# A modulation in part ahead of the first norm and in part between the projections

## The chip, the cores and the metric

The kernel runs on one core of a Trainium2 chip. The metric is the time of one execution on the device in microseconds (us).
## What is computed

Two layers of a backbone over 512 latent tokens and 256 context tokens of 1024 channels, in fp32. Each layer norms its tokens, scales and shifts them by a modulation (six vectors of 1024 for each of two layers, from the condition c for the latent and from c_ctx for the context tokens), mixes them, and adds the result; then the same with a feed-forward part. Layer 0 mixes by a two-directional recurrence over time (RWKV-7), layer 1 by attention. Cut to what matters here:

```python
mod_lat = einsum('bd,lde->lbe', silu(c), mod_w) + mod_b      # mod_w: (2 layers, 1024, 6144)
mod_ctx = einsum('d,lde->le', silu(c_ctx), mod_w) + mod_b
sh_m, sc_m, gt_m, sh_f, sc_f, gt_f = split(mod_lat[i], 6)    # and the same of mod_ctx
a = rms_norm(h, norm_mix[i]) * (1 + sc_m) + sh_m
xx = 0.5 * (previous token + next token of a) - a            # latent and context apart
xr, xw, xk, xv, xa, xg = (a + xx * mu[j] for j in range(6))
r, k, v = xr @ wr, xk @ wk, xv @ wv                          # and three small products of xw, xa, xg
```

## The kernel before

The program is a row of functions, each with its own block of instructions for every engine; at a block's end all engines meet at a barrier. Tokens are kept by channel: 8 channel tiles of 128 partitions, with 768 tokens (256 context, 512 latent) along the row.

`setup` (L113) issues 21 small loads on SP (the identity, the masks of the recurrence, the rows of parameters), and TensorE turns the parameter rows when all are there.

`modulation` (L178) goes over all of `mod_w` in 24 blocks of 512 columns (2 MB each, three buffers). Every block is split in two fp32r parts: ScalarE rounds it (`modw_hi`, L265), VectorE subtracts (`modw_lo`, L285). TensorE multiplies both parts, 16 matmuls of 512 columns, with the conditions as a stationary operand of four columns (L243, L244), ScalarE copies the result's rows, TensorE folds and turns them by channel (`fold`, L234), and VectorE adds the bias (L279). At the end VectorE makes all eight gains.

`load_tokens` (L309) loads the tokens by row (3 MB), turns them on TensorE with two pairs of banks in turn, copies them by channel, and spills them to DRAM. `norm_whole` (L354) takes the squares on ScalarE, sums them over the channels by matmuls with ones (L377), takes root and reciprocal, scales on VectorE and writes the normed tiles on ScalarE.

`rwkv_inputs` (L526) first makes the shifted difference `xx` of all tiles on VectorE (L675 to L681). Then three rounds follow: eight 128-column tiles of one large product and one small product each, 27 units. The order of the work is written out in `schedule` (L565), which every engine runs through with its own methods: `load` (SP, the weights two units ahead), `split` (ScalarE rounds, VectorE subtracts the weights of the next unit), `mix` (VectorE mixes a tile, L696, ScalarE rounds it, L719, GpSimd subtracts, L743), `product` (TensorE, 48 matmuls in three fp32r passes, L521 to L523) and `finish` (VectorE and ScalarE copy the result out of the banks, L702 and L724; SP waits for both copies, L634 and L635, and writes the tile to DRAM, L636). The mixes of an operand's first use stand ahead of its product; those of the next small product go along with the large one.

`recurrence` (L784) runs over head pairs; SP's `load(0)` at L1030, the load of `gate_w` behind it. After it come the output product, the feed-forward part, the attention, and another feed-forward part, whose weights pass through `SplitWeights` (L490) too.

Of the kernel before, what the change touches and what calls it, by code (L numbers as in the profile page):

```python
# [112 lines left out]
def setup(c, d):  # L113

    nc = c.nc
    with ExitStack() as ctx:
        rows = [ctx.enter_context(nc.sbuf_tensor(f"par_rows{n}", [P, P], F32)) for n in range(3)]
        loaded = ctx.enter_context(nc.semaphore("setup_loaded"))
        turned = ctx.enter_context(nc.semaphore("par_turned"))
        copied = ctx.enter_context(nc.semaphore("par_copied"))  # L120
        gated = ctx.enter_context(nc.semaphore("cond_silu"))
        row_of = lambda a: a.rearrange("(m p) -> m p", p=P)
# [11 lines left out]
        n_loads = 6 + sum(len(x) for x in lists)  # L134
        with nc.Block() as block:
            @block.sync
            def _(sp):
                for t, s in ((c.ident, "k_ident"), (c.ones_head, "k_ones_head"),
                             (c.score_mask, "k_score_mask"), (c.keep, "k_keep")):
                    sp.dma_start(t[:], d[s]).then_inc(loaded, 16)  # L140
                for h in range(2):
                    sp.dma_start(c.level_mask[half(h)], d["k_level_mask"][half(h)][:, :, :, half(h)]).then_inc(loaded, 16)
                for tile, parts in zip(rows, lists):
                    at = 0
                    for part in parts:
                        n = part.shape[0]
                        sp.dma_start(tile[at:at + n, :], part).then_inc(loaded, 16)
                        at += n

            @block.tensor  # L150
            def _(pe):
                pe.wait_ge(loaded, 16 * n_loads)
                for n, m in enumerate(sizes):
                    pe.transpose(c.bank[n][:, 0:m], rows[n][0:m, :], c.ident[0:m, 0:m]).then_inc(turned, 1)

            @block.vector
            def _(dve):
                at = 0
                nc.vector.memset(c.ones[:], 1.0).then_inc(copied, 1)
                nc.vector.memset(c.eps[:, 0:1], 1e-6).then_inc(copied, 1)  # L160
                nc.vector.memset(c.eps[:, 1:2], 64e-5).then_inc(copied, 1)
                dve.wait_ge(turned, 3)
                for n, m in enumerate(sizes):
                    at += CT if n == 2 else 0
                    nc.vector.tensor_copy(c.par[:, at:at + m], c.bank[n][:, 0:m]).then_inc(copied, 1)
                    at += m
                dve.wait_ge(copied, 6)

                nc.vector.tensor_scalar(c.par[:, PLESS:PLESS + CT], c.par[:, PKA:PKA + CT], -1.0, 1.0, ALU.mult, ALU.add)\
                    .then_inc(copied, 1)  # L170

            @block.scalar
            def _(act):
                act.wait_ge(copied, 6)
                nc.scalar.activation(c.cond[:], c.par[:, PC:PC + 16], ACT.Silu).then_inc(gated, 1)

def modulation(c, d):  # L178

    nc = c.nc
    W = 512
    BLOCKS = 2 * 6 * D // W
    BODY = 6
    with ExitStack() as ctx:
        sb = lambda n, s, dt=F32: ctx.enter_context(nc.sbuf_tensor(n, s, dt))  # L190
        sem = lambda n: ctx.enter_context(nc.semaphore(n))
        raw = [sb(f"modw{s}", [P, CT, W]) for s in range(3)]
        hi, lo = ([sb(f"modw_{n}{s}", [P, CT, W], F32R) for s in range(2)] for n in ("hi", "lo"))
        cond, cond_hi = sb("cond_parts", [P, CT, 4], F32R), sb("cond_hi", [P, CT, 4], F32R)
        fold, zeros = sb("fold", [4, 2]), sb("zeros", [P, CT, 4])
        row = [sb(f"modrow{s}", [4, W]) for s in range(2)]
        loaded = [sem(f"modw_loaded{s}") for s in range(3)]
        rounded, rest, product, copied, turned, stored = (sem(f"mod_{n}") for n in (
            "rounded", "rest", "product", "row_copied", "turned", "stored"))
        gains, fold_loaded, parts = sem("norm_gains"), sem("fold_loaded"), sem("cond_parts")  # L200
        src = d["mod_w"].rearrange("l (k p) e -> l p k e", p=P)

        def blocks(eng, step):

            for j in range(BODY):
                step(j, 0, j)
            with eng.Fori(1, BLOCKS // BODY) as i:
                for j in range(BODY):
                    step(BODY * i + j, i, j)

        with nc.Block() as block:
            @block.sync
            def _(sp):
                sp.dma_start(fold[:], d["k_fold"]).then_inc(fold_loaded, 16)
                per = BLOCKS // 2
                for l in range(2):
                    def step(n, cols, j):
                        need(sp, rest, n - 2)
                        sp.dma_start(raw[j % 3][:], src[l][:, :, cols]).then_inc(loaded[j % 3], 16)

                    if l == 0:
                        for j in range(BODY):
                            step(j, slice(j * W, j * W + W), j)
                    with sp.Fori(1 - l, per // BODY) as i:
                        for j in range(BODY):
                            step(per * l + BODY * i + j, bass.ds((BODY * i + j) * W, W), j)

            @block.tensor
            def _(pe):
                def turn(n, s):  # L230
                    pe.wait_ge(copied, n + 1)
                    need(pe, stored, n - 1)
                    for q in range(4):
                        mm = pe.matmul(c.bank[2 + s][:, 2 * q:2 * q + 2], row[s][:, q * P:(q + 1) * P], fold[:],  # L234
                                       start=True, stop=True)
                    mm.then_inc(turned, 1)

                def step(n, i, j):
                    s = j % 2
                    pe.wait_ge(rest, n + 1)  # L240
                    need(pe, copied, n - 1)
                    for k in range(CT):
                        pe.matmul(c.bank[s][0:4, :], cond[:, k, :], hi[s][:, k, :], start=(k == 0), stop=False)  # L243
                        mm = pe.matmul(c.bank[s][0:4, :], cond_hi[:, k, :], lo[s][:, k, :], start=False, stop=(k == CT - 1))  # L244
                    mm.then_inc(product, 1)
                    if not isinstance(n, int) or n:
                        turn(n - 1, 1 - s)

                pe.wait_ge(fold_loaded, 16)
                pe.wait_ge(parts, 4)  # L250
                blocks(pe, step)
                turn(BLOCKS - 1, 1)

            @block.scalar
            def _(act):
                def copy(n, s):
                    act.wait_ge(product, n + 1)
                    need(act, turned, n - 1)
                    signal(act, nc.scalar.copy(row[s][:], c.bank[s][0:4, :]), copied, n + 1)

                def step(n, i, j):
                    s = j % 2
                    act.wait_ge(loaded[j % 3], 16 * (BODY // 3 * i + j // 3 + 1))
                    need(act, product, n - 1)
                    nc.scalar.copy(hi[s][:], raw[j % 3][:]).then_inc(rounded, 1)  # L265
                    if not isinstance(n, int) or n:
                        copy(n - 1, 1 - s)

                blocks(act, step)
                copy(BLOCKS - 1, 1)  # L270

            @block.vector
            def _(dve):
                v = nc.vector

                def finish(n, s):
                    dve.wait_ge(turned, n + 1)
# [1977 lines left out]
```

## Time and profile before

| | us |
|---|---|
| median of 3 runs | 2885.71 (2883.48 to 2888.0) |
| the profiled execution | 2886.92 |
| its span, first to last instruction | 2885.1 |
| TensorE busy in the span | 2454.2 (85%) |
| VectorE busy | 1245.5 (43%) |
| ScalarE busy | 898.8 (31%) |
| GpSimd busy | 457.6 (16%) |
| granted TensorE clock, mean | 0.927 |

The page's first part gives these busy times, its second part the span in 40 slices. The busy share of an engine is a mean over stages that are limited by different things; which engine or transfer a stage waits for is read from that stage's own stretch. A line in a grouped view names the source line, the engine, the operation, output and inputs, shapes and count, then busy time and mean duration, then the idle time before it and what ended it. Matmuls are pipelined: the records of neighbours overlap, and an fp32 matmul that isn't fp32r leaves two records.

### The profile page before, as it was taken

The numbers are of one execution on the slowest core, as the hardware profiler recorded it, in microseconds if no ns is written. First come the engines' busy times: TensorE is split into PE (matmuls) and PEld (weight loads), VectorE is DVE, ScalarE is ACT, GpSimd is POOL, SyncE is SP. The second block draws the span as 40 slices with busy tenths as digits, with TensorE's granted clock in tenths as the row PEclk, the third lists the DMA queues.
The fourth block names the chain that finished last, engine by engine and source line by source line (L and its number), as shares of the span: only waits on it lengthen the run. The fifth ranks groups of instructions, "written<-read, shape, count | busy, mean of one in ns | idle before, by whom it ended". The sixth has DMA issues, their size and how long they took to land. (4 is left out here: it accounts for less than half of the span.)

```text
span 2885.1 us, 60344 instructions
## 1 busy us (share of the span) xinstructions
PE 2454.2 (85%) x26259; PEld 1985.4 (69%) x26259; DVE 1245.5 (43%) x1589; ACT 898.8 (31%) x1342; POOL 457.6 (16%) x335
## 2 busy tenths in 40 slices
PE   4863999759889888988697999999969676899999
PEld 1332877548887777878586888888856343588887
DVE  4656444245555555554234222222227654433333
ACT  4543233233233233332115321122143332443231
POOL 0001233053443444343000000000012000000000
PEclk9886999779999999999898999999989898999999
DMA  7751322200000000000122121222111001233332
GB/s 280 286 195 66 104 83 84 80 20 3 27 21 8 26 21 8 27 8 3 63 96 59 58 74 58 59 65 70 40 45 51 0 0 29 58 98 103 90 100 89
DMA packets 235966, 191.73 MB, mean 66 GB/s; under 512 B 10466, under 2 KB 201580, under 8 KB 235244
## 3 DMA queue, kind: packets, MB, share of 16 engines
q1 hardware_dynamic: 235756, 188.57, 20.6%
q8 instruction: 175, 2.87, 0.4%
q14 instruction: 35, 0.29, 0.0%
HBM read 170.73 MB, written 17.83 MB: 65 GB/s over the span
## 5 line engine op out<-in xcount | busy, mean ns | idle before, releaser
L515 DVE TENSOR_TENSOR ffn_lo<-ffn_raw,ffn_hi 128x1024 fp32r<-128x1024 f32 (+1 forms) x120 | 159.8, 1332 | 575.4 <-ACT ffn_hi L511 575.3
L521 PE MATMUL bank<-operand_hi,ffn_hi 128*128 128x512 f32 (+1 forms) x1056 | 379.3, 359 | 25.4 <-DVE operand_lo L486 25.4
L522 PE MATMUL bank<-operand_lo,ffn_hi 128*128 128x512 f32 (+1 forms) x1056 | 378.5, 358 | 0.0
L523 PE MATMUL bank<-operand_hi,ffn_lo 128*128 128x512 f32 (+1 forms) x1056 | 375.7, 356 | 0.0
L511 ACT CAST ffn_hi<-ffn_raw 128x1024 fp32r<-128x1024 f32 (+1 forms) x120 | 136.5, 1137 | 532.9 <-PE bank L523 532.7
L1472 POOL TENSOR_TENSOR lvl<-sc,level_mask 128x512 f32<-128x512 f32 x144 | 198.2, 1383 | 468.8 <-PE bank L1098 439.1
L521 PEld LDWEIGHTS bank<-operand_hi,ffn_hi 128*128 128x128 f32 x1056 | 200.7, 190 | 62.7 <-issue 22.2
L523 PEld LDWEIGHTS bank<-operand_hi,ffn_lo 128*128 128x128 f32 x1056 | 200.2, 190 | 29.9
L522 PEld LDWEIGHTS bank<-operand_lo,ffn_hi 128*128 128x128 f32 x1056 | 200.9, 190 | 27.3
L521 PE MATMUL bank<-mix_hi,proj_hi 128*128 128x256 f32 (+1 forms) x432 | 153.5, 355 | 56.4 <-POOL mix_lo L743 56.4
L522 PE MATMUL bank<-ffn_g_lo,ffn_hi 128*128 128x512 f32 (+1 forms) x528 | 188.0, 356 | 0.0
L521 PE MATMUL bank<-ffn_g_hi,ffn_hi 128*128 128x512 f32 (+1 forms) x528 | 187.5, 355 | 0.0
L523 PE MATMUL bank<-ffn_g_hi,ffn_lo 128*128 128x512 f32 (+1 forms) x528 | 186.7, 354 | 0.0
L1263 DVE TENSOR_TENSOR inverse<-bank,inverse 128x512 f32<-128x512 f32 x120 | 82.6, 688 | 178.4 <-PE bank L1107 178.1
L743 POOL TENSOR_TENSOR mix_lo<-mix_full,mix_hi 128x768 fp32r<-128x768 f32 (+1 forms) x48 | 87.9, 1832 | 439.4 <-ACT mix_hi L719 438.5
L522 PE MATMUL bank<-mix_lo,proj_hi 128*128 128x256 f32 (+1 forms) x432 | 151.8, 351 | 0.0
L523 PE MATMUL bank<-mix_hi,proj_lo 128*128 128x256 f32 (+1 forms) x432 | 150.2, 348 | 0.0
L1107 PE MATMUL bank<-inverse,t_sb 64*64 64x64 f32 x3840 | 135.3, 220 | 10.5 <-DVE inverse L1263 5.7
L1098 PE MATMUL bank<-inverse_t,lvl 64*64 64x64 f32 x3840 | 142.8, 228 | 0.8 <-DVE inverse_t L1257 0.7
L521 PEld LDWEIGHTS bank<-mix_hi,proj_hi 128*128 128x128 f32 x432 | 85.3, 197 | 76.2 <-issue 38.9
L243 PE MATMUL bank<-modw_hi,cond_parts 128*4 128x512 f32 x192 | 88.8, 463 | 53.5 <-DVE modw_lo L285 53.5
L1107 PEld LDWEIGHTS bank<-inverse,t_sb 64*64 64x64 f32 x3840 | 124.8, 137 | 13.4 <-DVE inverse L1263 6.7
(250 smaller groups left out, 4966.3 us busy)
## 6 DMA issues: line engine op xcount, KB each, us to landing
modw<-in_mod_w SPq DMA_DIRECT2D x24, 2048.0 KB, 8.5
ffn_raw<-in_ff_w SPq DMA_DIRECT2D x88, 512.0 KB, 3.8
ffn_raw<-in_ff_w SPq DMA_DIRECT2D x32, 704.0 KB, 4.6
proj_raw<-in_rw_wr SPq DMA_DIRECT2D x8, 512.0 KB, 3.9
proj_raw<-in_rw_wk SPq DMA_DIRECT2D x8, 512.0 KB, 4.1
proj_raw<-in_rw_wv SPq DMA_DIRECT2D x8, 512.0 KB, 4.0
rwkv_out_raw<-in_rw_wo SPq DMA_DIRECT2D x8, 512.0 KB, 3.6
qk_w_raw<-in_at_wq SPq DMA_DIRECT2D x8, 512.0 KB, 3.6
```

Source lines behind the costliest of these rows:

```text
L243: pe.matmul(c.bank[s][0:4, :], cond[:, k, :], hi[s][:, k, :], start=(k == 0), stop=False)
L511: signal(act, self.nc.scalar.copy(self.hi[s][:, 0:k_tiles, :], self.raw[s][:, 0:k_tiles, :]), self.rounded, n + 1)
L515: signal(eng, eng.tensor_tensor(self.lo[s][:, 0:k_tiles, :], self.raw[s][:, 0:k_tiles, :], self.hi[s][:, 0:k_tiles, :].bitcast(F32), ALU.s ...
L521: pe.matmul(out, w[0], x[0], start=first, stop=False)
L522: pe.matmul(out, w[0], x[1], start=False, stop=False)
L523: return pe.matmul(out, w[1], x[0], start=False, stop=last)
L743: signal(pool, nc.gpsimd.tensor_tensor(column(mix_lo[q % 2], k), full[s][:], column(mix_hi[q % 2], k).bitcast(F32), ALU.subtract), mix_res ...
L1098: mm = pe.matmul(T_BANK[half(h), w * CH:w * CH + CH], lvl[G.parity][n % 2][half(h), w, :], inv_t[G.parity][half(h), w, :], start=True, sto ...
L1107: mm = pe.matmul(X_BANK[half(h), w * CH:w * CH + CH], t_sb[G.parity][half(h), w, :], inv[G.third][half(h), w, :], start=True, stop=True)
L1263: v.tensor_tensor(y, X_BANK[:], y, ALU.add).then_inc(x_added, 1)
L1472: g.tensor_tensor(lvl[G.parity][n % 2][:].rearrange("p (q e) t -> p q e t", e=2), sc[G.third][:, :, :, 0, :], c.level_mask[:, n].unsqueeze ...
```

## The change

- `setup`, `modulation`, `load_tokens` and `norm_whole` become one function, `opening`, and a class `Modulation`. Blocks are 256 columns wide (48 of them, 1 MB each in two pieces of 512 KB) and are multiplied in plain fp32, without a split. The conditions are padded to 32 stationary columns, and the four channel tiles of a piece go to four column groups of the array (`tile_position=(0, 32 * j)`), whose parts are summed by the `fold` matmul when the row is turned.
- `opening` computes only blocks 0 to 7 (shift and scale of layer 0's mixer) ahead of the normed tiles, and blocks 8 and 9 among them.
- The first norm works by token: ScalarE sums the squares of the rows, the rows are scaled and then turned, and gain and shift are applied as they leave the banks. The unscaled tokens are turned too, for the spill, through one pair of banks.
- The other 38 blocks stand in `rwkv_inputs`: 10 to 15 among the first mixes (k < 6), 16 to 47 behind the units, one each and two in units 4, 8, 12, 17, 21 and 25. Every engine does its part of a block at that place in its own order: SP the loads, TensorE the turn of the block before and the product, ScalarE the copy, VectorE the store of the block before. Buffers there: three pieces.
- The shift is made tile by tile, ahead of the tile's first mix. The loops over pairs of units are unrolled.
- The masks of the recurrence are loaded in `recurrence`, behind `load(0)` and ahead of `gate_w`; VectorE and GpSimd wait for them at the start.
- `SplitWeights` has one set of semaphores for all stages, counted on from stage to stage.

```diff
+MOD_W = 256
+MOD_BLOCKS = 2 * 6 * D // MOD_W
+MOD_EARLY = 10
+class Modulation:
+    def load(self, sp, n, i):
+        piece = 2 * (n - self.first) + i
+        need(sp, self.product, piece - self.deep + 1)
+        l, at = n // (MOD_BLOCKS // 2), n % (MOD_BLOCKS // 2) * MOD_W
+        sp.dma_start(self.raw[piece % self.deep][:], self.src[l][:, 4 * i:4 * i + 4, at:at + MOD_W])\
+            .then_inc(self.loaded[piece % self.deep], 16)
+    def multiply(self, pe, n):
+        m = n - self.first
+        need(pe, self.copied, m)
+        for i in range(2):
+            piece = 2 * m + i
+            pe.wait_ge(self.loaded[piece % self.deep], 16 * (piece // self.deep + 1))
+            for j in range(4):
+                mm = pe.matmul(self.c.bank[6][32 * j:32 * j + 32, 0:MOD_W], self.c.cond[:, 4 * i + j, :],
+                               self.raw[piece % self.deep][:, j, :], start=(i == 0), stop=(i == 1),
+                               tile_position=(0, 32 * j))
+            mm.then_inc(self.product, 1)
+    def turn(self, pe, n):
+        m = n - self.first
+        pe.wait_ge(self.copied, m + 1)
+        need(pe, self.stored, m)
+        for q in range(2):
+            mm = pe.matmul(self.c.bank[7][:, 2 * q:2 * q + 2], self.row[:, q * P:(q + 1) * P], self.c.fold[:],
+                           start=True, stop=True)
+        mm.then_inc(self.turned, 1)
...
+def opening(c, d, a, spilled):
...
+        mods = Modulation(c, ctx, d, "mod0", 8)
...
+                sp.dma_start(xt[:, 0:2, :], d["ctx"][0].rearrange("(t p) e -> p t e", p=P)).then_inc(x_loaded[0], 16)
+                sp.dma_start(xt[:, 2:T, :], d["x"][0].rearrange("(t p) e -> p t e", p=P)).then_inc(x_loaded[1], 16)
...
+                for k in range(CT):
+                    need(pe, lat_copied, k)
+                    need(pe, ctx_copied, k)
+                    turn_x(xt, k, (c.bank[0], c.bank[1]), turned)
+                pe.wait_ge(gated, 1)
+                mods.multiply(pe, 0)
+                turn_rows(2)
+                mods.turn(pe, 0)
+                for n in range(1, 8):
+                    mods.multiply(pe, n)
+                    mods.turn(pe, n)
+                    if n == 4:
+                        pe.wait_ge(rows_copied, 2)
+                        turn_scaled(0), turn_scaled(1)
+                for k in range(2, CT):
+                    turn_scaled(k)
+                    if k % 3 == 2:
+                        n = 8 + k // 3
+                        if n < MOD_EARLY:
+                            mods.multiply(pe, n)
+                            mods.turn(pe, n)
...
 def rwkv_inputs
+        mods = Modulation(c, ctx, d, "mod1", 3)
+        mods.first = MOD_EARLY
...
+        AHEAD = 6
+        def mods_after(u):
+            rest = MOD_BLOCKS - MOD_EARLY - AHEAD
+            cuts = [MOD_EARLY + AHEAD + rest * i // (UNITS - 1) for i in range(UNITS)]
+            return list(range(cuts[u], cuts[u + 1])) if u + 1 < UNITS else []
...
             for k in range(CT):
                 E.mix(0, k, k % 2)
+                if k < AHEAD:
+                    E.mod(MOD_EARLY + k)
...
                         E.product(u, 2 * m, 2 * i + s)
                         E.finish(u, m, 2 * i + s)
-                pair(0)
-                with E.eng.Fori(1, CT // 2 - 1) as i:
-                    pair(i)
-                pair(CT // 2 - 1)
+                        for n in mods_after(u.n):
+                            E.mod(n)
...
+                        if k in (2, 5):
+                            for n in mods_after(u.n)[k // 3:k // 3 + 1]:
+                                E.mod(n)
...
                 class Sp(Part):
+                    def mod(self, n):
+                        for i in range(2):
+                            mods.load(sp, n, i)
...
                 class Pe(Part):
+                    def mod(self, n):
+                        if n > MOD_EARLY:
+                            mods.turn(pe, n - 1)
+                        mods.multiply(pe, n)
...
                 class Act(Part):
+                    def mod(self, n):
+                        mods.copy(act, n)
...
                 load(0)
+                sp.dma_start(keep[:], d["k_keep"]).then_inc(masks_loaded, 16)
+                sp.dma_start(score_mask[:], d["k_score_mask"]).then_inc(masks_loaded, 16)
+                for h in range(2):
+                    sp.dma_start(level_mask[half(h)], d["k_level_mask"][half(h)][:, :, :, half(h)]).then_inc(masks_loaded, 16)
                 sp.dma_start(gate_w[:], d["rw_g2"][0]).then_inc(slices[0], 16)
```

## Rows read from the trace of the kernel before

**Rows 1.** Stretches: length; PE, PEld, DVE, ACT, POOL busy; clock; DMA share; GB/s.

```profile
13.40:204.20 190.80, 136.98 (x576) 58.21 (x576) 110.59 (x61) 100.37 (x48) 0.00 (x0) 0.87 0.73 264
204.20:224.20 20.00, 8.27 (x48) 7.33 (x48) 5.53 (x8) 3.00 (x9) 0.00 (x0) 0.66 0.40 158
224.20:255.70 31.50, 12.28 (x32) 6.47 (x32) 12.62 (x9) 18.76 (x27) 0.00 (x0) 0.74 0.24 101
255.70:296.30 40.60, 14.52 (x49) 10.08 (x50) 32.22 (x29) 8.84 (x11) 14.52 (x8) 0.63 0.14 39
296.30:540.30 244.00, 229.58 (x1249) 196.31 (x1247) 97.70 (x88) 73.44 (x97) 73.42 (x40) 0.95 0.31 91
```

**Rows 2.** Groups by line and form within the modulation, 13 to 204 us.

```profile
L285 DVE TENSOR_TENSOR modw_lo<-modw,modw_hi 128x4096 fp32r<-128x4096 f32 x24 | 106.2, 4425 | 50.9 <-ACT modw_hi L265 50.5
...
L234 PE MATMUL bank<-fold,modrow 4*128 4x2 f32 x192 | 25.0, 249 | 0.0
```

**Rows 3.** Timeline of the token load: start, duration, engine, line, what.

```profile
204.22 0.38 SPq L322 DMA_DIRECT2D xt<-in_ctx  x1
...
214.32 1.97 PE L338 MATMUL bank<-ident,xt 128*128 128x128 f32 x8 [11.59 <-DMA xt<-in_x]
...
217.18 0.69 DVE L345 COPY tokens_in<-bank 128x512 f32<-128x512 f32 x1 [0.59 <-PE bank L338]
```

**Rows 4.** The same columns as rows 1, while modulation loads are queued up.

```profile
27.00:32.00 5.00, 2.00 (x5) 0.62 (x6) 4.08 (x2) 3.61 (x1) 0.00 (x0) 1.00 1.05 385
```

**Rows 5.** Timeline of ScalarE in the first norm, each square waiting for TensorE's sums.

```profile
231.00 0.84 ACT L386 ACTIVATE norm_sq<-tokens_in 128x768 f32<-128x768 f32 x1 [0.45 <-PE bank L377]
232.29 0.84 ACT L386 ACTIVATE norm_sq<-tokens_in 128x768 f32<-128x768 f32 x1 [0.45 <-PE bank L377]
```

**Rows 6.** Timeline of TensorE in the recurrence, one group of 64x64 matmuls.

```profile
701.94 1.10 PE L1107 MATMUL bank<-inverse,t_sb 64*64 64x64 f32 x32
```

**Rows 7.** Timeline of VectorE and GpSimd from 255 to 296 us.

```profile
255.81 7.02 DVE L675 TENSOR_TENSOR shifted<-normed 128x766 f32<-128x766 f32 x8 [1.65 <-PEq L367]
...
263.17 7.04 DVE L681 SCALAR_TENSOR_TENSOR shifted<-shifted,normed 128x768 f32<-128x768 f32 x8
...
281.01 3.67 DVE L696 SCALAR_TENSOR_TENSOR mix_full<-shifted,par,normed 128x768 f32<-128x768 f32 x2 [1.92 <-POOL mix_lo L743]
...
295.11 1.02 DVE L696 SCALAR_TENSOR_TENSOR mix_full<-shifted,par,normed 128x768 f32<-128x768 f32 x1
...
279.10 3.71 POOL L743 TENSOR_TENSOR mix_lo<-mix_full,mix_hi 128x768 fp32r<-128x768 f32 x2 [1.88 <-ACT mix_hi L719]
```

**Rows 8.** Timeline of a unit's end: evacuation, write and next load.

```profile
347.31 0.37 ACT L724 COPY proj_out<-bank 128x256 f32<-128x256 f32 x1 [3.42 <-PE bank L523]
347.32 0.69 DVE L702 COPY proj_out<-bank 128x512 f32<-128x512 f32 x1 [4.36 <-PE bank L523]
...
348.04 0.36 SPq L636 DMA_DIRECT2D r_all<-proj_out  x1
348.44 0.43 SPq L506 DMA_DIRECT2D proj_raw<-in_rw_wk  x1
```

**Rows 9.** From the view of the tile proj_raw: its 27 loads.

```profile
DMA to landing us min/median/max: 3.3/4.1/5.1
```

**Rows 10.** Timeline of TensorE in the modulation, after a pause.

```profile
44.69 0.59 PE L243 MATMUL bank<-modw_hi,cond_parts 128*4 128x512 f32 x1 [4.11 <-DVE modw_lo L285]
...
48.56 0.39 PE L243 MATMUL bank<-modw_hi,cond_parts 128*4 128x512 f32 x1
```

**Rows 11.** Timeline of VectorE: evacuations of units 7 and 9.

```profile
355.72 0.69 DVE L702 COPY proj_out<-bank 128x512 f32<-128x512 f32 x1 [4.58 <-PE bank L523]
...
383.87 0.69 DVE L702 COPY proj_out<-bank 128x512 f32<-128x512 f32 x1
```

**Rows 12.** Timeline: the setup's level-mask loads, and ScalarE in the recurrence.

```profile
2.61 1.34 SPq L142 DMA_DIRECT2D level_mask<-in_k_level_mask  x2
...
548.34 0.93 ACT L1397 ACTIVATE tmp<-k_pair,par 128x768 f32<-128x768 f32 x1 [8.28 <-DMA gate_w<-in_rw_g]
```

More of the change, by code:

```diff
@@ L133, in setup, with rows_load @@
         sizes = [114, 120, 32]
-        n_loads = 6 + sum(len(x) for x in lists)
+        LAT_SLOT, CTX_SLOT = slice(0, LAT), slice(0, CTX)
+        def rows_load(eng, n):
+            at = 0
+            for part in lists[n]:
+                eng.dma_start(rows[n][at:at + part.shape[0], :], part).then_inc(rows_loaded[n], 16)
+                at += part.shape[0]
         with nc.Block() as block:
@@ L137, in _ @@
             def _(sp):
[L138 to L148, printed above, removed]
+                sp.dma_start(c.ident[:], d["k_ident"]).then_inc(first_loaded, 16)
@@ L150, in _ @@
+                sp.wait_ge(lat_copied, CT)
+                sp.wait_ge(ctx_copied, CT)
+                sp.dma_start(spilled, h[:]).then_inc(c.spilled, 16)
+                sp.wait_ge(c.spilled, 16)
             @block.tensor
             def _(pe):
[L152 to L270, printed above, removed]
@@ new lines, in turn_rows, with turn_x @@
+                def turn_rows(n):
+                    pe.wait_ge(rows_loaded[n], 16 * (len(lists[n]) + (1 if n == 1 else 0)))
+                    pe.transpose(c.bank[n][:, 0:sizes[n]], rows[n][0:sizes[n], :], c.ident[0:sizes[n], 0:sizes[n]])\
+                        .then_inc(rows_turned, 1)
+                def turn_x(src, k, banks, done):
+                    for t in range(T):
+                        out = banks[0][:, t * P:(t + 1) * P] if t < 2 else banks[1][:, (t - 2) * P:(t - 1) * P]
+                        mm = pe.transpose(out, src[:, t, k * P:(k + 1) * P], c.ident[:])
+                    mm.then_inc(done, 1)
@@ new lines, in _ @@
+                for k in range(2, CT):
+                    dve.wait_ge(turned, k + 1)
+                    v.tensor_copy(h[:, k, CTX:TOK], c.bank[1][:, LAT_SLOT]).then_inc(lat_copied, 1)
+                copy_rows(2, PNM)
+                for n in range(8):
+                    mods.store(dve, n)
+                dve.wait_ge(mods.stored, 8)
+                dve.wait_ge(rows_copied, 2)
+                for r in range(2):
+                    mods.gain(v, 0, 0, PNM, r).then_inc(gains, 1)
+                dve.wait_ge(gains, 2)
@@ new lines, in _ @@
+                act.wait_ge(consts, 4)
+                act.wait_ge(rows_copied, 1)
+                nc.scalar.activation(c.cond[:, :, 0:2].rearrange("p k r -> p r k"),
+                                     c.par[:, PC:PC + 16].rearrange("p (r k) -> p r k", k=CT), ACT.Silu).then_inc(gated, 1)
+                for t in range(T):
+                    if t in (0, 2):
+                        act.wait_ge(x_loaded[t // 2], 16)
+                    nc.scalar.activation(xs[:, t, :], xt[:, t, :], ACT.Square, accum_out=squares[:, t:t + 1]).then_inc(squared, 1)
+                    if t < 2:
+                        act.wait_ge(turned, t + 1)
+                        nc.scalar.copy(h[:, t, 0:CTX], c.bank[0][:, CTX_SLOT]).then_inc(ctx_copied, 1)
@@ new lines, in _ @@
+                act.wait_ge(squared, T)
+                nc.scalar.activation(std[:], squares[:], ACT.Sqrt, scale=1.0 / D, bias=c.eps[:, 0:1]).then_inc(rooted, 1)
+                for k in range(2, 5):
+                    act.wait_ge(turned, k + 1)
+                    nc.scalar.copy(h[:, k, 0:CTX], c.bank[0][:, CTX_SLOT]).then_inc(ctx_copied, 1)
+                act.wait_ge(inverted, 1)
+                for t in range(1, T, 2):
+                    nc.scalar.activation(xs[:, t, :], xt[:, t, :], ACT.Copy, scale=std[:, t:t + 1]).then_inc(scaled_act, 1)
@@ new lines, in _ @@
+                for k in range(5, CT):
+                    act.wait_ge(turned, k + 1)
+                    nc.scalar.copy(h[:, k, 0:CTX], c.bank[0][:, CTX_SLOT]).then_inc(ctx_copied, 1)
+                for n in range(8):
+                    mods.copy(act, n)
+                act.wait_ge(gains, 2)
+                for k in range(CT):
+                    act.wait_ge(s_turned, k + 1)
+                    nc.scalar.activation(a[:, k, 0:CTX], c.bank[2 + 2 * (k % 2)][:, CTX_SLOT], ACT.Identity,
+                                         scale=c.gain[:, 0, 0, 1, k:k + 1], bias=c.mod[:, 0, k, 1:2]).then_inc(a_ctx, 1)
+                    if k % 3 == 2 and 8 + k // 3 < MOD_EARLY:
+                        mods.copy(act, 8 + k // 3)
@@ L569, in schedule @@
                 E.mix(0, k, k % 2)
+                if k < AHEAD:
+                    E.mod(MOD_EARLY + k)
             for m in range(3):
                 base = (CT + 1) * m
-                def pair(i):
+                for i in range(CT // 2):
                     for s in range(2):
@@ L597, in nothing @@
                 pass
-            load = split = mix = product = finish = finish_small = nothing
+            load = split = mix = product = finish = finish_small = mod = nothing
         def column(t, k):
@@ L631, in where @@
                         return m, u.n - m * (CT + 1)
+                    def mod(self, n):
+                        for i in range(2):
+                            mods.load(sp, n, i)
                     def finish(self, u, m, tile):
@@ L705, in _ @@
                 schedule(Dve())
+                mods.store(dve, MOD_BLOCKS - 1)
+                dve.wait_ge(mods.stored, MOD_BLOCKS - MOD_EARLY)
+                for l in range(2):
+                    for kind, base in ((0, PNM), (1, PNF)):
+                        for r in range(2):
+                            if l or kind:
+                                mods.gain(v, l, kind, base, r).then_inc(gains, 1)
             @block.scalar
@@ L1566, in add @@
                 def add(m, s):
[L1567 removed]
+                    dve.wait_ge(w.product, w.at + m + 1)
                     for q, (at, width) in enumerate(segs):
```

329 lines of the change are left out of this document (157 added, 172 removed).

## The prediction

> **What bounds the kernel now.** I read the stages first: the page gives shares of the whole span, so I cut the trace into stretches by stage [rows 1]. After some 13 us of tables, 190.8 us go to the modulation, 20.0 to loading and turning the tokens, 31.5 to the first norm, 40.6 to the start of the time-mix inputs (up to the first projection tile's end at 296.3) and 244.0 to the other 26 products. All engines pass a barrier between these functions, so their lengths add up. The modulation is set by splitting: 24 blocks, one VectorE subtraction of 4.425 us each behind a ScalarE cast that it waits for, 106.2 us busy and 50.9 idle [rows 2]; its matmuls have air. The 244.0 us behind 296.3 are TensorE's: 229.6 busy, at 0.95 of full clock. So time taken from the front counts whole, and whatever is put on TensorE's path between two projections counts whole as well, with what TensorE has to wait for there. Behind the projections stands the recurrence, which the change touches only in when its masks are loaded; the later stages get other semaphore numbers and nothing else, which I cost at nothing.
>
> **The front, shortened.** SP now issues the token loads near 3.5 us. Before, TensorE could use them 10.1 us after the issue [rows 3], so they are there at about 14 us. A channel tile is six transposes (1.3 us a tile: the copy of 0.69 and the 0.59 that it waited [rows 3]) and a copy of 0.69 us, and with one pair of banks instead of two they no longer overlap: with the hand-overs 2.2 us, times 8 = 17.6. Between the second and the third tile VectorE waits for ScalarE's six squares and root, then scales three rows; that holds the banks some 7 us longer. Turned: 14 + 17.6 + 7 = 38.5 us. Only then the first block is multiplied; four blocks have landed long since (385 GB/s were reached with loads queued up [rows 4], 1 MB in 2.7 us), and each later one is asked for when a piece is freed, some 10 us ahead of its use, so DMA is not the bound.
>
> A block is 8 plain fp32 matmuls over 256 columns. The old norm's ones-matmuls show the price of plain fp32: 768 columns in 1.29 us at full clock [rows 5], so 0.43 us each and 3.4 us a block one after the other. The four of a piece lie in different column groups of the array. The nearest row is the recurrence's 64x64 pairs in opposite quadrants: 32 records (16 matmuls of 64 columns, 1.7 us in a row at that price) took 1.10 us with their tail [rows 6], so about two at a time. I take two: 1.7 us a block at full clock, 3.4 at half; bounds 0.85 and 3.4 at full clock. The turning adds a copy (0.37 for that shape [rows 8]), three hand-overs (0.3) and four records of 0.13 (192 took 25.0 us [rows 2]): 1.2 us with nothing beside it, because here the turn follows its own product at once. So 2.9 us a block, 4.8 at half clock, and with TensorE half idle I take 3.8: eight blocks 30, two pairs of scaled transposes 2.4, at 71 us. Then eight channel tiles at 1.3 us with two more blocks among them, less the two tiles turned ahead: 16, and the last parameter rows with the barrier 1.5. The time-mix inputs begin at **88 us** (78 to 102, by the bounds of the block) instead of 255.7. The 3 MB that are spilled go out when the last block's load is issued (near 58) and are done by about 76, so the block's end is not theirs.
>
> **The time-mix inputs to their first product.** VectorE now subtracts the first weight tile ahead of the shift (6.3 us, mostly the wait for the load, which the shift used to cover). A column tile then costs the shift 0.95 + 0.9 + small copies and waits, 2.1 us [rows 7], and the mix 1.0, and GpSimd's 1.85 us come on top, since a VectorE mix beside it takes 1.83 instead of 1.02 us [rows 7]: about 5.1 us a tile. Six blocks (10 to 15) lie between; with three buffers of half a block they turn over in some 5 us and keep pace. 6.3 + 8 x 5.1 + 3 = **50 us** (38 if VectorE and GpSimd didn't hinder each other, 55 if the blocks come last) against 40.6. The first product ends at 88 + 50 = 138 instead of 296.3: **158 us gained** (139 to 180).
>
> **The 32 blocks between the projections: the price.** SP works in order. In a unit it waits for both evacuations of that unit's product, writes the tile out, and *only then* issues the loads of the block that TensorE multiplies right behind that same product. Nothing asks for the block earlier, so its load is exposed each time. From a unit of before: evacuation begins at 347.32, the write is issued at 348.04, the next load at 348.44 [rows 8], 1.2 us after the product's end. A 512 KB load behind such a write lands 4.1 us after its issue (3.3 to 5.1) [rows 9]: the first piece at +5.2, the second 1.4 later at +6.6. TensorE, idle for 5 us, is at half clock then: a pause of 4.11 us was followed by matmuls of 0.59 us, and 3.9 us later they took 0.39 [rows 10]. Two pieces at half clock: 1.7 each, +6.9 and +8.6; the next product runs its first part at half clock, 0.4. So **9.0 us a unit**, over 24 units: 216. Bounds: fastest landing and four matmuls at a time 7.3; one at a time 10.8 (3.4 for the first, 2.1 for the second as the clock comes back). The turn of the block before lies in the wait and costs nothing; without that wait 0.5.
>
> Four of these units (4, 12, 21, 25) carry a second block, whose last piece can be asked for only when the first piece is used up: +3.6 each, 14. In the two small units (8, 17) loads run ahead, as nothing is written there; but the casts of the mix now wait on ScalarE behind a copy that waits for TensorE, and VectorE behind the store. From unit 7's end to unit 9's takes 28.2 us now [rows 11], of which 11 are TensorE waiting for the mixes; with all that chained I get 36.9, +8.7, so they take no more than the 9.0 that unit 7 is charged. Behind ScalarE's copy there queues the rounding of the weights two units on, needed 8 us later: covered. VectorE's store is 0.16 us and SP's later weight load has a unit in hand. Stalls: 216 + 14 = **230 us** (183 to 279).
>
> **The recurrence's start.** Four mask loads (1 MB) now stand between the first pair's slices and the gate weights, and ScalarE's first operation waits for those: 8.28 us after the barrier before [rows 12]. Four issues (1.34 us for the two of the level mask [rows 12], so at most 2.7 in all) and 1 MB at 385 GB/s: 2 to 5, I take **3.5** (0 to 8; not below nothing, as nothing there is taken away).
>
> **Sum.** -158 + 230 + 3.5 = +75.5. Profiled execution 2886.9 (span 2885.1 and 1.8 around it) gives 2962.4; the median of the runs is 1.2 below the profiled one: **2961 us**, 2.6% slower.
>
> **The rivals.** *Four at a time.* The column groups may run together, not by twos. Rows: only pairs are shown. Then 8.5 instead of 9.0 us a unit (-12) and 0.85 us less for ten blocks (-8.5): 2940. The Trainium skill ("TensorE: Matmul & The Clock Gate", Part 3) states this: tiles in different column groups run concurrently, with 2.38 times for three; no run here shows it yet. *One at a time.* Then +1.8 x 24, +1.7 to 2.5 for each of ten early blocks: +63, 3024; a front that stays 25 us longer for other reasons lands near 2990. *Faster: the loads are hidden.* If the next block's data were there when a product ends (the mechanism: SP runs ahead of TensorE by a unit), a block costs its matmuls and turn, 1.7 + 0.5 for 32 = 70: 2887 - 158 + 70 + 3.5 - 1 = 2802. It speaks against it that SP's wait for the evacuation stands ahead of the loads. It decides where the stall falls under (158 - 3.5 - 14) / 24 = 5.9 us a unit, which even the fastest landing (+4.5 for the first piece alone, the second at +5.8, then its matmuls) doesn't reach. *The change doesn't do what it says*: a front that still waits for more than eight blocks; nothing in the diff has it wait so.
>
> **How the numbers follow.** The forecast with matmuls by twos 0.52 (its own range 2925 to 2990), four at a time 0.15, one at a time or a longer front 0.17, hidden loads 0.11, landing and front both at their best ends 0.05 (about 2890 to 2905, no change to slightly slower). A run tells about 0.2% (6 us) from no change. Faster 0.12 (hidden loads and a little of the last), same 0.03, slower 0.85. The range runs from the best ends, 2895, to the one-at-a-time case, 3022, and leaves out the hidden loads and both outer tails.
>
> **What would show it.** In the profile after: projections beginning near 88 us and the first product's end near 138; in the stage behind it TensorE idle for 5 to 6 us ahead of each block's matmuls, released by the DMA of the block's weights; granted clock of that stage well under the 0.95 of now, as each pause ends at half clock; a unit of 17 to 18 us instead of 8.4; the stage 475 us long instead of 244. The starts of the four matmuls of a piece tell whether they run by ones, twos or fours. Pauses under 3 us ahead of the blocks, or SP issuing their loads before the evacuation, would prove the central step wrong; a first product's end after 165 the front.

## The result

The changed kernel takes 2967.1 us, median of four runs (2961.3 to 2971.4), against 2884.6 us beside it: 1.0283 times the time before, 95% interval 1.0263 to 1.0303. The profiled execution, with a span of 2959.5 us, is the fastest of the four, 5.8 us under the median.

Cut by the same stages as rows 1: to the barrier ahead of the time-mix inputs, to the first product's end, to the recurrence's barrier, and to ScalarE's first operation in the recurrence (columns as in rows 1):

```profile
0.00:75.80 75.80, 42.54 (x299) 27.73 (x299) 17.11 (x41) 23.46 (x45) 0.20 (x4) 0.89 0.66 225
75.80:125.00 49.20, 28.00 (x166) 16.67 (x167) 40.95 (x56) 11.13 (x17) 14.53 (x8) 0.62 0.54 161
125.00:615.40 490.40, 339.96 (x1891) 253.83 (x1891) 103.84 (x127) 82.64 (x129) 73.84 (x40) 0.78 0.38 114
615.40:627.35 11.95, 0.00 (x0) 0.00 (x0) 0.91 (x6) 0.00 (x0) 0.00 (x0) 0.54 0.96 274
```

The first product ends at 125.0 instead of 296.3, 171.3 us earlier. The stage behind it is 490.4 us long instead of 244.0 [rows 1], so 246.4 us are lost there. TensorE's idle time in it went from 14.4 to 150.4 us, and its granted clock from 0.95 to 0.78. The two groups that the change put into this stage, and what its matmuls wait for (grouped view of TensorE from 125.0 to 615.4 us):

```profile
L148 PE MATMUL bank<-mod_raw,cond 128*32 128x256 f32 x512 | 65.0, 602 | 140.9 <-DMA mod_raw<-in_mod_w 140.9
...
L159 PE MATMUL bank<-fold,mod_row 128*128 128x2 f32 x131 | 19.4, 252 | 3.2 <-ACT mod_row L168 3.2
```

Who waited longest in the same stretch (engine and line, for whom: us in total, times, longest):

```profile
POOL mix_lo L756 <- ACT mix_hi L729: 393.6, 33, 21.2
ACT mod_row L168 <- PE bank L148: 200.9, 30, 8.8
DVE proj_lo L485 <- ACT proj_hi L480: 191.6, 25, 9.6
PE bank L148 <- DMA mod_raw<-in_mod_w: 140.9, 52, 6.9
```

The first three are engines that stand behind TensorE and are not late. ScalarE's wait for the block is new, and VectorE's wait for ScalarE grew from 30.9 us in the same stretch of before; TensorE itself waits only 5.3 us for GpSimd and 3.2 us for ScalarE here. The fourth is the price.

That closes the account of the stage: 136 us more idle (141 of waiting for the blocks' weights, less 7 of waiting for mixes, and small change), 65.0 and about 19 for the blocks' matmuls and turns, and the products, busy 256 us instead of 229.6: 26 us of half clock. 136 + 65 + 19 + 26 = 246.

One unit shows how (timeline from unit 3's evacuation to unit 4's; the place of rows 8):

```profile
179.64 0.69 DVE L705 COPY proj_out<-bank 128x512 f32<-128x512 f32 x1 [6.38 <-PE bank L494]
...
180.48 0.34 SPq L623 DMA_DIRECT2D r_all<-proj_out  x1
180.87 1.12 SPq L137 DMA_DIRECT2D mod_raw<-in_mod_w  x2
...
185.29 1.08 PE L148 MATMUL bank<-mod_raw,cond 128*32 128x256 f32 x8 [5.40 <-DMA mod_raw<-in_mod_w]
...
186.73 1.08 PE L148 MATMUL bank<-mod_raw,cond 128*32 128x256 f32 x8 [0.35 <-DMA mod_raw<-in_mod_w]
...
197.37 0.69 DVE L705 COPY proj_out<-bank 128x512 f32<-128x512 f32 x1 [5.82 <-PE bank L494]
```

Evacuation, write, and only then the loads; TensorE gets the first piece 5.65 us after the evacuation began, the second at 7.1, and the next product begins at 8.1. Unit to unit it is 17.7 us here. Over the 18 such intervals with one block the mean is 18.2 us instead of 8.4.

### The profile page after: what moved, and what is told of

It reads as the page before. It is cut to its first block and busy times, and to the rows that moved or that the text cites. A ratio compares the mean times of both kernels' runs of the same rounds, so it can differ in the third digit from the quotient of the medians.

```text
span 2959.5 us, 60881 instructions
## 1 busy us (share of the span) xinstructions
PE 2455.8 (83%) x26659; PEld 2000.0 (68%) x26659; DVE 1147.6 (39%) x1611; ACT 810.6 (27%) x1340; POOL 457.8 (15%) x335
## 5 line engine op out<-in xcount | busy, mean ns | idle before, releaser
L148 PE MATMUL bank<-mod_raw,cond 128*32 128x256 f32 x768 | 92.5, 587 | 150.8 <-DMA mod_raw<-in_mod_w 150.7
L492 PE MATMUL bank<-mix_hi,proj_hi 128*128 128x256 f32 (+1 forms) x432 | 167.8, 388 | 10.0 <-POOL mix_lo L756 10.0
L756 POOL TENSOR_TENSOR mix_lo<-mix_full,mix_hi 128x768 fp32r<-128x768 f32 x48 | 88.4, 1841 | 501.8 <-ACT mix_hi L729 501.3
L493 PE MATMUL bank<-mix_lo,proj_hi 128*128 128x256 f32 (+1 forms) x432 | 161.4, 374 | 0.0
L494 PE MATMUL bank<-mix_hi,proj_lo 128*128 128x256 f32 (+1 forms) x432 | 158.7, 367 | 0.0
L148 PEld LDWEIGHTS bank<-mod_raw,cond 128*32 128x32 f32 x768 | 21.6, 138 | 187.1 <-issue 131.7
```

Source lines behind the costliest of these rows:

```text
L148: mm = pe.matmul(self.c.bank[6][32 * j:32 * j + 32, 0:MOD_W], self.c.cond[:, 4 * i + j, :], self.raw[piece % self.deep][:, j, :], start=(i ...
L492: pe.matmul(out, w[0], x[0], start=first, stop=False)
L493: pe.matmul(out, w[0], x[1], start=False, stop=False)
L494: return pe.matmul(out, w[1], x[0], start=False, stop=last)
L756: signal(pool, nc.gpsimd.tensor_tensor(column(mix_lo[q % 2], k), full[s][:], column(mix_hi[q % 2], k).bitcast(F32), ALU.subtract), mix_res ...
```

## The experiments

The theory behind the prediction: the loss is the exposed load of each block, set by SP's order, with half clock as an addition. Its rivals: the loads cost by sharing the DMA engines, wherever they stand; other parts of the edit (unrolled loops, the shift by tile, common semaphores) cost as well; the blocks' matmuls are the price.

**The loads ahead of the wait** (e1). This puts them ahead of the unit's write too; a later experiment tries the write alone.

```diff
 (schedule, in each large unit)
+                        for n in mods_after(u.n):
+                            E.early(n)          # SP alone: the two loads of block n
                         E.finish(u, m, 2 * i + s)
                         for n in mods_after(u.n):
                             E.mod(n)            # SP: nothing for a block already asked for
```

> SP issues a unit's block loads ahead of its wait for that unit's evacuation, everything else as in the changed kernel. Theory (the exposed load is the cost): TensorE's 141 us of waiting for the blocks' weights in the 490 us stage go, the clock stays up (26 us less on the products, 30 less on the blocks' matmuls), about 304 us for the stage and 2781 us in all. Rival (the loads cost because they share the DMA engines with weights and writes): under 60 us gained, over 2900.

Measured: 2784.2 us, 0.9646 of the kernel before (0.9630 to 0.9662); 183 us less than the changed kernel. The stage, then SP and TensorE about one product's end at 198.1 us:

```profile
130.40:438.10 307.70, 285.96 (x1891) 231.63 (x1891) 103.17 (x128) 82.70 (x129) 73.43 (x40) 0.94 0.60 178
```

```profile
198.88 0.34 SPq L632 DMA_DIRECT2D r_all<-proj_out  x1
199.27 0.43 SPq L475 DMA_DIRECT2D proj_raw<-in_rw_wk  x1
...
198.34 1.07 PE L148 MATMUL bank<-mod_raw,cond 128*32 128x256 f32 x16
...
207.85 0.50 PE L159 MATMUL bank<-fold,mod_row 128*128 128x2 f32 x4
208.28 1.07 PE L148 MATMUL bank<-mod_raw,cond 128*32 128x256 f32 x16
```

The stage is 307.7 us (304 expected) at a clock of 0.94; behind the product's end SP has only the write and the next weights to issue, a whole block is one row now, 1.07 us with no wait and ahead of SP's write, and the unit 9.93 us. What is left of waiting, 14.5 us instead of 140.9, comes seven times. The same bytes pass at 178 GB/s instead of 114. So sharing the DMA engines isn't the price; the order is. The change's idea is worth 103 us over the kernel before once two loads stand ahead of one wait.

**The 32 blocks left out** (e4).

```diff
         def mods_after(u):
...
-            return list(range(cuts[u], cuts[u + 1])) if u + 1 < UNITS else []
+            return []
```

> Blocks 16 to 47 are left out (their modulation stays zero), all else as in the changed kernel. Theory (the whole loss sits in what stands behind the units): the stage falls back to about 244 us, 2721 us in all. Rival (unrolled loops, the shift tile by tile or the common semaphores cost something too): the stage stays over 260, over 2740.

Measured: 2718.8 us (ratio 0.942, 0.9398 to 0.9441), and the stage is

```profile
126.80:370.70 243.90, 229.70 (x1252) 196.55 (x1251) 98.75 (x95) 73.34 (x97) 73.30 (x40) 0.95 0.32 91
```

243.9 us against 244.0 in rows 1, with the same busy times. In this stage unrolling and the common semaphores cost nothing that can be seen; what stands behind the units costs the 248 us between this kernel and the changed one. The shift by tile isn't tested by it: it stands ahead of the first product, and that stretch takes 49.3 us here, 49.2 in the changed kernel and 40.6 before, with six blocks and the first weights' split in it too. No run takes these apart.

**The write behind the loads** (e2).

```diff
 (SP, large unit)
                         sp.wait_ge(evac_lat, CT * m + tile + 1)
                         sp.wait_ge(evac_ctx, CT * m + tile + 1)
-                        sp.dma_start(column(dram[m], tile), out[u.s][:]).then_inc(kept, 16)
...
                             E.mod(n)
+                        E.write(u, m, 2 * i + s)    # the dma_start of above
```

> SP still waits for the evacuation, but issues the block's loads ahead of the write of the unit's tile. Theory (the write's issue of 0.4 us and its 384 KB, 1.0 us, stand ahead of the block in the queue): 1.4 us a unit over 24 units, 34 us less, 2933. Rival (the landing is latency, not queueing): the issue alone, 9 us less, 2958.

Measured: 2971.3 us (1.0293, 1.0276 to 1.0310), nothing gained; I had expected 34 us. A unit of it (evacuation, loads, the block's two pieces):

```profile
183.18 0.69 DVE L708 COPY proj_out<-bank 128x512 f32<-128x512 f32 x1 [6.06 <-PE bank L494]
184.01 0.92 SPq L137 DMA_DIRECT2D mod_raw<-in_mod_w  x2
...
188.06 1.08 PE L148 MATMUL bank<-mod_raw,cond 128*32 128x256 f32 x8 [4.64 <-DMA mod_raw<-in_mod_w]
...
190.00 1.08 PE L148 MATMUL bank<-mod_raw,cond 128*32 128x256 f32 x8 [0.86 <-DMA mod_raw<-in_mod_w]
```

The first piece is there after 4.9 us instead of 5.65, but the second after 6.8 instead of 7.1. Over the 18 units with one block the next product begins 7.8 us after the evacuation instead of 8.0, so 0.2 us earlier and not 1.4. The DMA packets in the traces show why the write was cheap where it stood (means over these 18 units): its packets ran from 0.8 to 2.2 us after its issue, before the first packet of the pieces, which came 1.8 us after their own issue. With the write behind them the pieces' first packet comes after 1.0 us, but their packets then take 4.5 us in all instead of 3.4. The write's packets overlap only the last 1.2 us of that, and why the pieces slow down already before isn't shown. The transfers landed in the order of their issue in both kernels; the write, now behind the pieces, lands 6.0 us after its issue instead of 2.9. Even the 0.2 us a unit don't reach the end: the clock comes back between 9.6 and 13.8 us after the evacuation in either kernel, in the mean 11.3 in the changed one and 11.5 here, and the unit takes 18.3 us instead of 18.2.

**Spare matmuls in the waits** (e5). To price the clock by itself:

```diff
 (TensorE, between the turn and the block's product)
+                        for _ in range(22):
+                            pe.matmul(c.bank[4][:, 0:P], c.ones[:], c.ident[:], start=True, stop=True)
                         mods.multiply(pe, n)
```

> 22 spare matmuls of 128 columns in plain fp32 (about 4.7 us) run on TensorE in every wait for a block, into a bank that nobody reads. Theory (half clock is a part of the price): blocks' matmuls 65 to 35 us and products 26 us shorter, about 50 less, 2917. Rival (only the wait counts, the clock doesn't): 2967, no change.

Measured: 2971.7 us (1.0296, 1.0279 to 1.0313), which looks like the rival. It isn't. The block's pieces at full clock:

```profile
184.23 0.64 PE L148 MATMUL bank<-mod_raw,cond 128*32 128x256 f32 x8 [1.19 <-DMA mod_raw<-in_mod_w]
...
185.69 0.64 PE L148 MATMUL bank<-mod_raw,cond 128*32 128x256 f32 x8 [0.83 <-DMA mod_raw<-in_mod_w]
```

and of the 18 units with one block twelve took 16.0 to 16.4 us, where the changed kernel's mean is 18.2; the other six took 16.7 to 19.0, and the mean was 16.8. The spare work also ran where nothing is waited for, ahead of second blocks (units with two blocks took 23.4 to 27.5 us instead of 20.8 to 23.0) and of the blocks of the small units (41 and 42 us over the turn of a round, instead of 36 and 38). So once more, with the spare matmuls only in the units with one block (e8):

> The changed kernel with e5's spare matmuls, but only in the units with one block. Theory (half clock costs 2.0 us a unit, and e5 gave it back in the units with two blocks and the small ones, where the spare matmuls stood in the way): 20 units by 2.0, 2927 to 2931. Rival (the shorter units of e5 are paid for elsewhere): 2967.

Measured: 2947.7 us (1.0200, 1.0171 to 1.0229), 19 us less than the changed kernel, with 16.8 us a unit in the mean over the same 18 intervals. The stage in this kernel:

```profile
127.30:593.30 466.00, 402.67 (x2773) 334.64 (x2771) 103.67 (x127) 82.84 (x129) 73.39 (x40) 0.93 0.40 120
```

466 us instead of 490, at 0.93 instead of 0.78; the busy time holds the spare matmuls. Half clock is real, about 2 us in a unit where it is avoided whole. But in two of the 18 units the first piece landed 7.0 us after the evacuation instead of 5.2 to 6.0, the spare work had ended by then, and the clock fell (19.4 us each); so the stage gave 24 of the expected 36 to 40 us, and the whole execution 19. Half clock is a part of the price and the smaller one: 2 of the 9.8 us that a unit lost.

**One column group** (e7). On the kernel with the early loads, all eight matmuls of a block in one group:

```diff
-                mm = pe.matmul(self.c.bank[6][32 * j:32 * j + 32, 0:MOD_W], self.c.cond[:, 4 * i + j, :],
-                               self.raw[piece % self.deep][:, j, :], start=(i == 0), stop=(i == 1),
-                               tile_position=(0, 32 * j))
+                mm = pe.matmul(self.c.bank[6][0:32, 0:MOD_W], self.c.cond[:, 4 * i + j, :],
+                               self.raw[piece % self.deep][:, j, :], start=(i == j == 0), stop=(i == 1 and j == 3),
+                               tile_position=(0, 0))
```

> As e1_ahead, but all eight matmuls of a block go to the first column group, one after another (the other rows of the fold are zero). Theory (a block took 1.07 us because four column groups run together; alone a matmul of 256 columns takes 0.43 us): 3.4 us a block at full clock, 2.35 more for 48 blocks less those that lie beside the mixes, 95 more, 2880. Rival (the records' 1.07 us isn't overlap, a plain fp32 matmul with 32 stationary columns is short by itself): within 10 us of e1_ahead.

Measured: 2858.1 us (0.9902, 0.9887 to 0.9917), 74 us more than with four groups. A block at full clock:

```profile
53.91 3.64 PE L152 MATMUL bank<-mod_raw,cond 128*32 128x256 f32 x16
```

3.64 us against the 1.07 of the row from the early loads. So the four groups do run together. A unit went from 9.93 to 12.50 us. What is missing from my 95 stands chiefly in two places: units with two blocks took 17.2 to 17.3 us, about as they had with four groups (16.4 to 17.5), where TensorE had waited for the load instead, and the front grew by 14 us for its ten blocks, as all but the first ran at full clock now.

**The masks behind the gate weights** (e6), on the kernel with the early loads:

```diff
                 load(0)
+                sp.dma_start(gate_w[:], d["rw_g2"][0]).then_inc(slices[0], 16)
                 sp.dma_start(keep[:], d["k_keep"]).then_inc(masks_loaded, 16)
...
-                sp.dma_start(gate_w[:], d["rw_g2"][0]).then_inc(slices[0], 16)
                 load(1)
```

> As e1_ahead, and the masks of the recurrence are loaded behind the gate weights instead of ahead of them. Theory (ScalarE's first operation waits for the gate weights, 12.0 us behind the barrier instead of 8.0): back to about 8 us, 4 us less, 2780. Rival (VectorE and GpSimd wait for the masks anyway and are needed as early): no change, 2784.

Measured: 2779.2 us (0.9634, 0.9617 to 0.9651), 5 us less than e1, within what two such runs differ by. The profile shows the step: the barrier at 433.59 and ScalarE 8.0 us behind it, as before the change, where the changed kernel took 12.0:

```profile
441.56 0.93 ACT L1426 ACTIVATE tmp<-k_pair,par 128x768 f32<-128x768 f32 x1 [8.49 <-DMA gate_w<-in_rw_g]
```

**No second blocks in large units** (e9), on top of that:

```diff
-        AHEAD = 6
+        AHEAD = 8
...
-            rest = MOD_BLOCKS - MOD_EARLY - AHEAD
-            cuts = [MOD_EARLY + AHEAD + rest * i // (UNITS - 1) for i in range(UNITS)]
+            small = (CT, 2 * CT + 1)
+            cuts = [MOD_EARLY + AHEAD + i + 2 * sum(s < i for s in small) for i in range(UNITS)]
...
-                        if k in (2, 5):
+                        if k in (2, 5, 7):
```

> As e6_ahead_masks, and the four second blocks of large units go elsewhere: eight blocks instead of six among the first mixes, three instead of two in the small units 8 and 17, one everywhere else. Theory (with three buffers a second block's last piece can only be asked for when the first is used: such a unit took 16.4 to 17.5 us in e1 against 9.93): 26 us less there, about 8 more at the start and in the small units, 2762. Rival (the blocks cost the same wherever they stand): 2780.

Measured: 2757.8 us (0.9557, 0.9542 to 0.9572). All 21 intervals between large units of one round are 9.91 to 9.94 us. From the first product's end, here 133.0 us (it comes later by the two blocks more ahead of it), to the barrier:

```profile
133.00:416.10 283.10, 270.69 (x1851) 223.00 (x1851) 102.55 (x125) 81.43 (x126) 71.50 (x39) 0.97 0.62 186
```

283 us instead of e1's 308, at a clock of 0.97. Of the 39 us over the 244.0 of rows 1, some 32 are the 21 units' 1.5 us each (1.07 for the block, the rest about its turn), which can't go as long as TensorE bounds the stage; 7 stand in the two passages from one round to the next, with four blocks each.

**Two pairs of banks for the tokens** (e10), and the kernel of e9 once more beside it (e11):

```diff
-                    need(pe, lat_copied, k)
-                    need(pe, ctx_copied, k)
-                    turn_x(xt, k, (c.bank[0], c.bank[1]), turned)
+                    need(pe, lat_copied, k - 1)
+                    need(pe, ctx_copied, k - 1)
+                    turn_x(xt, k, (c.bank[4 * (k % 2)], c.bank[4 * (k % 2) + 1]), turned)
```

> As e9_spread, and the unscaled tokens are turned through two pairs of banks in turn, as load_tokens did, instead of one. Theory (transposes and copies don't overlap with one pair: 2.32 us a tile in the changed kernel, 1.5 of it transposes; the front's chain runs through them): 0.8 us a tile for five or six tiles, 4 us less, 2754. Rival (the hold by ScalarE's root and scaling sets the end of the turning anyway): no change, 2758.

> The kernel of e9_spread once more beside e10, so that the two can be compared on one chip. Expected: 2758, as in its first run, whichever theory holds.

Measured: 2753.4 us (0.9538, 0.9525 to 0.9551) and, for the second, 2755.3 (0.9542, 0.9527 to 0.9556). In the profile of e10 the first block begins with

```profile
31.67 1.85 PE L148 MATMUL bank<-mod_raw,cond 128*32 128x256 f32 x16
```

at 31.7 instead of 38.0 us, and the first product ends at 127.8 against 130.3 in e11 (and 133.0 in e9, the same kernel). But the intervals of the two times overlap: whether the pair of banks gains at all stays open. Either is 4.6% faster than the kernel before.

## Why the prediction was right

2961 us were forecast and 2967 measured, with the sign and the mechanism as given: each block's load is exposed behind SP's wait, as e1 shows. That the two numbers lie 6 us apart is luck, as two larger errors nearly met. By its steps:

- *The front* was the least exact one: 88 us forecast, 75.8 measured, just under its range of 78 to 102; the same front took 77.4 to 81.3 us in the other kernels that have it, about the range's lower end. The turning ended where I had it (38.5 and 38.0), but the eighth block's turn at 62.5 and not 71. The term that was too large is the block: I took the four groups by twos from the diagonal pairs of rows 6. In the changed kernel:

```profile
40.81 1.07 PE L148 MATMUL bank<-mod_raw,cond 128*32 128x256 f32 x16
...
46.28 1.93 PE L148 MATMUL bank<-mod_raw,cond 128*32 128x256 f32 x16
```

  1.07 us at full clock and 1.93 at half, instead of 1.7 and 3.4; with the turn 2.1 and 3.4 us a block from start to start. The Trainium skill's page "TensorE: Matmul & The Clock Gate" (Part 3) was the better guide here: it says that tiles in different column groups run concurrently. These traces agree: 1.07 us with four groups, 3.64 with one. The likeliest case should have been the rival with four at a time, and not matmuls by twos with 0.52 against 0.15; its own price, 2940, would have missed by 27 us, as it kept the small term for the clock.
- *To the first product*: 50 us forecast, 49.2 measured. The tile-by-tile shift does alternate with GpSimd: a copy of two elements that takes 0.16 us by itself stands for 1.78 while GpSimd subtracts, and the next tile's copies likewise, so a tile takes five us (VectorE, two tiles):

```profile
84.30 1.02 DVE L699 SCALAR_TENSOR_TENSOR mix_full<-shifted,par,normed 128x768 f32<-128x768 f32 x1
85.36 1.02 DVE L675 TENSOR_TENSOR shifted<-normed 128x254 f32<-128x254 f32 x2
86.29 0.16 DVE L677 COPY shifted<-normed 128x2 f32<-128x2 f32 x1
86.36 1.78 DVE L678 COPY shifted<-normed 128x2 f32<-128x2 f32 x1
...
89.17 1.02 DVE L699 SCALAR_TENSOR_TENSOR mix_full<-shifted,par,normed 128x768 f32<-128x768 f32 x1
```

- *The gain* was thus 171.3 us in this execution, not 158. Its front was the shortest of all with this code; in e1 the first product ends at 130.4, which is a gain of 166.
- *The stall a unit*: 9.0 forecast, 9.8 measured (18.2 less 8.4). The wait was right: first piece at +5.2 forecast, +5.2 to +6.0 measured. The product begins at +8.0 rather than +8.6, since the blocks are cheaper. What was too small is half clock, 0.4 us in the sum: a unit from the product's begin to its end takes 10.2 us, 1.8 more than 8.4, and e5's undisturbed units are 2.0 shorter. I had counted the clock's return from the block's first matmul, 3.9 us on as in rows 10; in the 18 units it came back 9.7 to 13.3 us after the evacuation, 5.8 us after that matmul in the mean. In rows 10 TensorE is busy without a gap, and here the block's first matmuls are followed by a further wait; that this makes the difference isn't tested.
- *Second blocks*: +3.6 forecast, 21.9 against 18.2 measured. *The small units*: from unit 7's end to unit 9's 36.4 us measured, 36.9 forecast; the second time 37.8.
- *The stage*: +230 forecast, +246.4 measured. *The recurrence's start*: +3.5 and +3.9; the rows are the masks' issues ahead of the gate weights':

```profile
617.90 0.43 SPq L1046 DMA_DIRECT2D keep<-in_k_keep  x1
618.37 0.43 SPq L1047 DMA_DIRECT2D score_mask<-in_k_score_mask  x1
618.84 1.35 SPq L1049 DMA_DIRECT2D level_mask<-in_k_level_mask  x2
620.24 0.98 SPq L1050 DMA_DIRECT2D gate_w<-in_rw_g  x1
...
627.35 0.93 ACT L1417 ACTIVATE tmp<-k_pair,par 128x768 f32<-128x768 f32 x1 [12.47 <-DMA gate_w<-in_rw_g]
```

- The sum by the trace is -171.3 + 246.4 + 3.9 = +79.0; the span grew by 74.4. The 4.6 us between them lie behind ScalarE's first operation in the recurrence, 2336.8 us before and 2332.2 after. That part of the code is the same in all kernels here and took 2337.1 us in e1: it varies by itself. The medians lie 82.5 us apart, as the profiled execution of the changed kernel is its fastest one and that of the kernel before lies 2.3 us above its median.

So two errors of 13 and 16 us, with opposite signs, nearly met. The rival on the other side, hidden loads, was given 2802 us; e1 built it and took 2784: the first product ended 166 us earlier and not 158, and the stage took 64 us more and not 70. A block at 1.07 us and not 1.7 makes both smaller, and the second blocks, at 16.4 to 17.5 us a unit, take a part of it back.

## What to carry to other kernels

When work is threaded into a loop whose order is written out for all engines, look at the queue that issues its loads first: a load placed at the same point as its use, behind a wait for the work just ahead of it, is exposed in full each time, however idle the DMA engines are (busy 0.38 of this stage). Ask where each engine will be when it reaches the new step, and issue the load one step earlier in the issuing engine's order. Price a pause of TensorE with the half clock that follows it (about 2 us behind each wait here), and spread such steps so that no unit needs more buffers than there are.

## What the runs showed of the hardware

- Moving a 384 KB write from ahead of two 512 KB loads to behind them, in one queue, made the write land 6.0 instead of 2.9 us after its issue and the second load only 0.2 us earlier in the mean (6.8 instead of 7.0 us after the evacuation). The landings kept the order of issue in both, but packets of the write and the second load overlapped by 1.2 us in e2.
- Plain fp32 matmuls with 32 stationary columns in four column groups: eight over 256 columns in 1.07 us, in one group 3.64 us.
- The same code in the front took 75.8 us in one execution and 81.0 in another (e1), by which of its blocks, turns and transposes ran at full clock: a block takes 1.07 or 1.93 us, a turn's matmuls 0.61 or 1.01.
